# The delta-rule branch's short convolution and Silu, moved from its head loop into the input projection

## What is computed

```
proj = h @ w_in                                   # c_qkv: 3 x 1024 columns of it
qkv = jax.nn.silu(causal_short_conv(c_qkv, gdn_conv))
q_c = l2norm(qkv[..., :C_KEY] by head) * (C_DK ** -0.5)
k_c = l2norm(qkv[..., C_KEY:2 * C_KEY] by head)
v_c = qkv[..., 2 * C_KEY:]
o_c = gated_delta_rule(q_c, k_c, v_c, log_a_c, beta_c)

def causal_short_conv(x, w):                      # 4 taps along the tokens, one weight per channel
    xp = jnp.pad(x, ((0, 0), (kw - 1, 0), (0, 0)))
    return sum(xp[:, j:j + t_len] * w[j] for j in range(4))
```

## Time and profile before

| | us |
|---|---|
| median of 3 runs | 4563.6 |
| runs | 4560.57 to 4564.49 |
| span of the profiled execution | 4562.1 |
| TensorE busy | 4115.5 (90%) |
| VectorE busy | 2743.6 (60%) |
| ScalarE busy | 1845.1 (40%) |
| GpSimd busy | 747.8 (16%) |

### The profile page before, as it was taken

One profiled execution on the slowest core, in us unless ns is written; L12 is line 12 of the kernel. 1 busy time (PEld: TensorE's weight loads), 2 busy tenths in 40 slices (PEclk: granted clock), 3 DMA queues, 4 the chain that ended last, 5 costly groups with the idle time before them and its releaser, 6 DMA issues. The chain is left out here.

```text
span 4562.1 us, 66543 instructions
## 1 busy us (share of the span) xinstructions
PE 4115.5 (90%) x26381; PEld 3202.9 (70%) x26381; DVE 2743.6 (60%) x3549; ACT 1845.1 (40%) x3376; POOL 747.8 (16%) x831
## 2 busy tenths in 40 slices
PE   7999889889988979999999999688689968999997
PEld 1888667668856767888888786465378854788786
DVE  1413777651277756555655654687577756666789
ACT  0312465531145643222222332787566623433533
POOL 0200400020040011000101200576212112222001
PEclk9999999999999989999999999799799989999998
DMA  7434411134331122332323232222301038224232
GB/s 268 163 110 156 145 61 49 55 128 151 111 136 58 49 107 79 102 120 85 128 93 117 95 120 79 66 67 76 112 31 53 25 128 315 88 102 157 103 128 79
DMA packets 257763, 489.79 MB, mean 107 GB/s; under 512 B 33992, under 2 KB 70056, under 8 KB 257212
## 3 DMA queue, kind: packets, MB, share of 16 engines
q1 hardware_dynamic: 257472, 485.80, 30.5%
HBM read 345.74 MB, written 140.00 MB: 106 GB/s over the span
## 5 line engine op out<-in xcount | busy, mean ns | idle before, releaser
L1028 DVE TENSOR_TENSOR p_tl<-spare,p_th 128x1024 fp32r<-128x1024 f32 x156 | 199.4, 1279 | 362.6 <-ACT p_th L900 362.6
L900 ACT CAST p_th<-spare 128x1024 fp32r<-128x1024 f32 x156 | 163.6, 1049 | 570.4 <-PE p_ps L852 570.4
L316 PE MATMUL p_ps<-p_wh,hi 128*128 128x512 f32 x896 | 352.7, 394 | 5.8 <-DVE p_wl L484 5.8
L316 PE MATMUL p_ps<-p_wl,hi 128*128 128x512 f32 x896 | 350.6, 391 | 0.0
L316 PE MATMUL p_ps<-p_wh,lo 128*128 128x512 f32 x896 | 350.5, 391 | 0.0
L852 PE MATMUL p_ps<-p_th,p_xh 128*128 128x512 f32 x784 | 310.6, 396 | 2.0 <-DVE p_tl L1028 2.0
L852 PE MATMUL p_ps<-p_th,p_xl 128*128 128x512 f32 x784 | 310.3, 396 | 0.0
L852 PE MATMUL p_ps<-p_tl,p_xh 128*128 128x512 f32 x784 | 310.3, 396 | 0.0
L852 PE MATMUL p_ps<-p_xh,p_th 128*128 128x512 f32 x672 | 266.2, 396 | 1.0 <-DVE p_tl L1028 1.0
L852 PE MATMUL p_ps<-p_xl,p_th 128*128 128x512 f32 x672 | 265.3, 395 | 0.0
L852 PE MATMUL p_ps<-p_xh,p_tl 128*128 128x512 f32 x672 | 264.1, 393 | 0.0
(11 more groups left out here) (485 smaller groups left out, 10551.4 us busy)
## 6 DMA issues: line engine op xcount, KB each, us to landing
spare<-w_in SPq DMA_DIRECT2D x56, 1024.0 KB, 5.5
p_raw<-w_in SPq DMA_DIRECT2D x40, 1024.0 KB, 5.9
pn_dram<-p_stg SPq DMA_DIRECT2D x128, 256.0 KB, 2.1
p_dram<-p_stg SPq DMA_DIRECT2D x112, 256.0 KB, 2.1
m_w<-w_mod SPq DMA_DIRECT2D x12, 2048.0 KB, 11.5
pt_dram<-p_stg SPq DMA_DIRECT2D x96, 256.0 KB, 2.2
zm_ogm<-pn_dram SPq DMA_DIRECT2D x48, 512.0 KB, 10.1
zu_raw<-w_up SPq DMA_DIRECT2D x16, 1024.0 KB, 5.4
```

What stands on the lines that cost most here:

```text
L316: mm = pe.matmul(ps[:, u, :], lhsT, rhs, start=(kk == 0 and q == 0), stop=(kk == KD - 1 and q == 2))
L900: act.copy(th[:, g % 2], (R11, T, R21, R12, R22, R11, R21)[i][:, 2 * u:2 * u + 2]).then_inc(s_hi, 1)
L1028: dve.tensor_tensor(tl[:, g % 2], (R11, T, R21, R12, R22, R11, R21)[i][:, 2 * u:2 * u + 2], th[:, g % 2], ALU.subtract).then_inc(s_lo, 1)
```

## The change

The convolution and Silu of the 24 (stream, head) pairs become 24 jobs inside the projection, behind units 0, 3, 6 and 9 of groups 6 to 12 (from unit 6 of group 6 to unit 3 of group 12). A job loads one 128x1024 row block from `pt_dram` into `rows`, does tap 0 on ScalarE, taps 1 and 2 on VectorE, tap 3 on GpSimd (a multiply in place and an add), Silu on ScalarE behind the second unit after it, and stores the block back. Its result lies in `C.low`, so what was there goes to `low_dram` and is loaded back at the end. The weights' columns are made in the modulations and kept in `C.cw`. The delta branch loads finished rows, in two buffers. The narrow columns are loaded and split in the projection, behind the rows, before its chain of sums.

```diff
 # modulations: ScalarE, VectorE lose the narrow split, SP its two loads; added:
+            sp.dma_start(cr[:], ins["gdn_conv_2"][0].rearrange("j (s p) -> (j s) p", p=P)).then_inc(s_cr, 16)
+            pe.wait_ge(s_cr, 16)
+            pe.transpose(psC[:], cr[:], C.ident[0:96, 0:96]).then_inc(s_cc, 1)
+            dve.wait_ge(s_cc, 1)
+            dve.tensor_copy(C.cw[:].rearrange("p j s h -> p (j s h)"), psC[:])
 # seven_products
+    PAD, JOBS = 16, 3 * C_HEADS
+        rows = sb("rows", [P, PAD + SEQ])
+        cv = C.low
+        conv_q = [q for q in range(NQ) if groups[q]["conv"] is not None]
+        spots = [(q, p) for q in range(conv_q[0] + 1, NQ) for p in (0, 3, 6, 9)][2:2 + JOBS]
+        job_at = {UN * q + p: n for n, (q, p) in enumerate(spots)}
+        weight = lambda n, tap: C.cw[:, tap, n // C_HEADS, n % C_HEADS:n % C_HEADS + 1]
+        taken = lambda tap: rows[:, PAD - 3 + tap:PAD - 3 + tap + SEQ]
 # SP, behind the head gains' loads
+                sp.dma_start(narrow[:, :, 0:RANK], wv[:, :, B_GK:B_GK + RANK]).then_inc(s_narrow, 16)
+                sp.dma_start(narrow[:, :, RANK:2 * RANK], wv[:, :, C_A:C_A + 2 * C_HEADS]).then_inc(s_narrow, 16)
 # SP
+            def load_rows(n):
+                if n % C_HEADS == 0:
+                    for b in range(SG):
+                        sp.wait_ge(s_st[b], 16 * ((PLAIN + 16 * (conv_q[n // C_HEADS] + 1)) // SG))
...
+                else:
+                    sp.wait_ge(s_cv, n)
+                r = groups[conv_q[n // C_HEADS]]["out"]
+                sp.dma_start(rows[:, PAD:], r[n % C_HEADS * P:(n % C_HEADS + 1) * P, :]).then_inc(s_rl, 16)
+            def store_rows(q, p):
+                n = job_at.get(UN * q + p)
+                if n is None:
+                    return
+                if n + 1 < JOBS:
+                    load_rows(n + 1)
+                sp.wait_ge(s_cs, n + 1)
+                r = groups[conv_q[n // C_HEADS]]["out"]
+                sp.dma_start(r[n % C_HEADS * P:(n % C_HEADS + 1) * P, :], cv[:]).then_inc(s_cst, 16)
+            sp.wait_ge(s_eA, 2 * NB // 2 + 2)
+            sp.dma_start(C.low_dram, cv[0:2 * RANK, :]).then_inc(s_low, 16)
             for q in range(NQ):
                 for i, freed in ((2, ((1, 8), (3, 10))), (4, ((0, 12),)), (5, ((2, 14),)), (6, ())):
+                    if (q, i) == (spots[0][0], 2):
+                        load_rows(0)
+                    for p in {2: (0, 3), 4: (6,), 5: (9,), 6: ()}[i]:
+                        store_rows(q, p)
                     for j in range(4):
                         store(q, i, j)
...
+            sp.wait_ge(s_cst, 16 * JOBS)
+            sp.dma_start(cv[0:2 * RANK, :], C.low_dram).then_inc(s_low, 16)
+            sp.wait_ge(s_low, 32)
 # ScalarE; behind the first two unit_hi: act.copy(narrow_hi[:], narrow[:])
+            def first_tap(n):
+                act.wait_ge(s_rl, 16 * (n + 1))
...
+                    act.wait_ge(s_cst, 16 * n)
+                act.activation(cv[:], taken(0), ACT.Identity, scale=weight(n, 0)).then_inc(s_tap, 1)
+            def rows_activated(n):
+                act.wait_ge(s_cv, n + 1)
+                act.activation(cv[:], cv[:], ACT.Silu).then_inc(s_cs, 1)
                 unit_hi(g + 2)
+                if g - 2 in job_at:
+                    rows_activated(job_at[g - 2])
                 if u == 1:
...
+                if g in job_at:
+                    first_tap(job_at[g])
 # GpSimd; head_gains(q, p) are the four tiles of unit p
+            def last_tap(n):
+                pool.wait_ge(s_tapD, n + 1)
+                pool.tensor_scalar(taken(3), taken(3), weight(n, 3), None, ALU.mult)
+                pool.drain()
+                pool.tensor_tensor(cv[:], cv[:], taken(3), ALU.add).then_inc(s_cv, 1)
             for q in range(NQ):
                 gain = groups[q]["gain"]
+                for p in range(UN):
+                    if p - 1 in (5, 9, 11) and gain is not None:
+                        head_gains(q, p - 1)
+                    if UN * q + p in job_at:
+                        last_tap(job_at[UN * q + p])
                 if gain is not None:
+                    head_gains(q, UN - 1)
 # VectorE; behind the first two unit_lo: narrow_lo = narrow - narrow_hi. In the loop, last:
+            def middle_taps(n):
+                dve.wait_ge(s_tap, n + 1)
+                for tap in (1, 2):
+                    e = dve.scalar_tensor_tensor(cv[:], taken(tap), weight(n, tap), cv[:], ALU.mult, ALU.add)
+                    if tap == 1:
+                        dve.drain()
+                e.then_inc(s_tapD, 1)
+                if g in job_at:
+                    middle_taps(job_at[g])
 # gated_delta: taps, silu, conv_v, conv_qk and all their calls and waits go; the turns read the loaded rows
-            pe.transpose(ps[:, 2, 0:96], cr[:], C.ident[0:96, 0:96]).then_inc(s["conv_cols"], 1)
             def load(h):
+                if h >= 2:
+                    sp.wait_ge(s["tokens"], 3 * (h - 1))
                 for q in range(3):
                     r0 = T_C + q * D + h * P
-                    sp.dma_start(raw[:, q, PAD:PAD + SEQ], C.pt_dram[r0:r0 + P, :]).then_inc(s["raw"], 16)
+                    sp.dma_start(cv[:, h % 2, q], C.pt_dram[r0:r0 + P, :]).then_inc(s_cv[h % 2], 16)
             load(0)
-            sp.wait_ge(s["conv"], 1)
-            sp.wait_ge(s["conv_v"], 1)
             load(1)
+                    pe.wait_ge(s_cv[g % 2], 48 * (g // 2 + 1))
                     for c in range(NCK):
-                        mm = pe.transpose(chunk(6, c), cv[:, step, c * CK:(c + 1) * CK], C.ident[:])
+                        mm = pe.transpose(chunk(6, c), cv[:, g % 2, step, c * CK:(c + 1) * CK], C.ident[:])
```

More of the change, by code:

```diff
@@ L139, in _ @@
                              .rearrange("p (a b) -> p a b", a=4)).then_inc(s_lv, 16)
-            wv = ins["w_in_2"][0].rearrange("(k p) n -> p k n", p=P)
-            with nc.allow_non_contiguous_dma("4 KB of channel gains each; 64-byte rows, 128 KB in all"):
+            with nc.allow_non_contiguous_dma("4 KB of channel gains each"):
                 sp.dma_start(C.mix_scale[:, 0, :], ins["ln_mix_pre_2"][0].rearrange("(k p) -> p k", p=P)).then_inc(s_late, 16)
@@ L624, in seven_products @@
         xh[5], xl[5] = sb("xh5", [P, KH, CH], F32R), sb("xl5", [P, KH, CH], F32R)
+        ms = sb("ms", [P, NT])
+        rs = sb("rs", [P, NT])
+        with ExitStack() as early:
+            narrow = sb("narrow", [P, KD, 2 * RANK], F32, early)
+            narrow_hi = sb("narrow_hi", [P, KD, 2 * RANK], F32R, early)
+            narrow_lo = sb("narrow_lo", [P, KD, 2 * RANK], F32R, early)
+        rows = sb("rows", [P, PAD + SEQ])
+        cv = C.low
         wh, wl = (xh[4], xh[3]), (xl[4], xl[3])
@@ L728, in _ @@
                 sp.dma_start(on[:], ins[name][0].partition_broadcast(P)).then_inc(s_on, 16)
+            wv = ins["w_in_2"][0].rearrange("(k p) n -> p k n", p=P)
+            with nc.allow_non_contiguous_dma("64-byte rows, 128 KB in all"):
+                sp.dma_start(narrow[:, :, 0:RANK], wv[:, :, B_GK:B_GK + RANK]).then_inc(s_narrow, 16)
+                sp.dma_start(narrow[:, :, RANK:2 * RANK], wv[:, :, C_A:C_A + 2 * C_HEADS]).then_inc(s_narrow, 16)
             for kh in range(2):
@@ L929, in _ @@
             unit_hi(1)
+            act.wait_ge(s_narrow, 32)
+            act.copy(narrow_hi[:], narrow[:]).then_inc(s_nh, 1)
             act.wait_ge(s_lA, NT)
@@ L1077, in _ @@
             unit_lo(1)
+            dve.wait_ge(s_nh, 1)
+            dve.tensor_tensor(narrow_lo[:], narrow[:], narrow_hi[:], ALU.subtract).then_inc(s_nl, 1)
             dve.wait_ge(s_T, NT)
@@ L2540, in gated_delta @@
         s_st = [sem(f"head_stored{b}") for b in range(2)]
+        s_cv = [sem(f"convolved_loaded{b}") for b in range(2)]
         block = st.enter_context(nc.Block())
@@ L2678, in take_o @@
                 act.copy(o[:, h % 2, c], ps[:, 3, 0:CK]).then_inc(s["o_taken"], 1)
-            taps(0, (0, 1))
-            taps(0, (2,))
             gates()
-            for q in (0, 1, 2):
-                silu(0, q)
             for step in (-2, -1, 1, 0):
@@ L2687, in _ @@
             rows(0, 0)
-            taps(1, (0, 1))
-            taps(1, (2,))
             for step in (3, 4):
@@ L3915, in second_block @@
                 pt, pn = C.pt_dram, C.pn_dram
-                token = lambda a, c, act=None, gain=None: dict(w=w[:, a:a + D], out=pn[:, c:c + D], kind="token", act=act, gain=gain)
+                token = lambda a, c, act=None, gain=None: dict(w=w[:, a:a + D], out=pn[:, c:c + D], kind="token", act=act, gain=gain, conv=None)
                 silu = lambda j: dict(act=ACT.Silu, gain=C.onorm[j][:])
-                channel = lambda a, r, act=None: dict(w=w[:, a:a + D], out=pt[r:r + D, :], kind="channel", act=act, gain=None)
+                channel = lambda a, r, act=None, conv=None: dict(w=w[:, a:a + D], out=pt[r:r + D, :], kind="channel", act=act, gain=None, conv=conv)
```

(2 more changed lines are left out.)

149 lines of the change are left out of this document (42 added, 107 removed).

## The result

The changed kernel takes 4530.1 us (median of 4 runs, 4526.8 to 4533.4), the kernel before 4562.1 on the same chip: a ratio of 0.9929, 95% interval [0.9917, 0.9941], 32 us less. The forecast was 4563, range 4541 to 4580. The result lies outside it.

A forecast was written before the change was run, and what follows sets the result against it. TensorE bounds the projection; the delta branch leaves it partly idle. Summed -47 (delta branch) + 22 (unit 3) + 16 (unit 9 with gains) + 5.6 (unit 9 elsewhere) + 3 (small parts) = -0.4 us: 4563 median, range 4541 to 4580.

The forecast's parts named there:

- the delta branch: Taps and Silus leave this stage: 47 us less (37 to 59), of which 4.0 for each of five heads.
- the start: Start of the delta branch: gates, first rows and key masking no longer wait behind taps and Silu, 20 us less (16 to 22).
- the 7: First head of the delta branch, with more TensorE idle than steady heads: 7 us less (4 to 9).
- The floor named there: Delta branch: the seventh head, which has no taps, takes 45.0 us between system products, against 50.7 with taps.
- the job behind unit 3: Projection, groups 7 to 12: two taps delay T4, then GpSimd's multiply and add block VectorE; six jobs, 22 us more.
- the multiply: GpSimd's 128x1024 multiply by a column in each job, shown nowhere in the trace at this size, taken as 1.5 us.
- Rival 1: T4 precedes GpSimd's multiply behind unit 3: 12 us less, another 4 with tl(13) first in groups 10, 11; 4547 us; chance 0.35.
- mere sharing: If GpSimd and VectorE only shared bandwidth, without a lock, unit 3 would lose the overrun alone, some 20 us less in all.
- rival 2: GpSimd's multiply costs as much as its add or more; a visible loss from 2.3 us; 4573 us; chance 0.24.
- the wait behind unit 9 with gains: Projection, groups 8 and 9: GpSimd's last tap delays gains, stores and the next block 0; 8 us each, 16 more (10 to 22).
- The other jobs: Unit 9 elsewhere: tl(13) loses 0.7 us in groups 6, 7 and 2.1 in 10, 11, 5.6 more; units 0 and 6: 0.
- Small parts: Narrow columns, transpose and copy of conv columns, and reloading the low rows (2.1 us): together 3 us more.

The follow-up runs named there:

- e13: Changed kernel with VectorE waiting for its own taps' semaphore and draining before T4 in the six jobs behind unit 3: 4528.4 us, ratio to before 0.9923.
- e4_no_jobs: Changed kernel with none of the 24 jobs issued, so no convolution or Silu, all else kept: 4495.0 us, ratio to before 0.9852.
- e5: Changed kernel with the two jobs behind unit 9 of groups 8 and 9 moved to units 6 and 9 of group 12: 4507.5 us, ratio to before 0.9887.
- e1: Kernel before with only the two 32-byte tiles ms and rs allocated behind xh5 and xl5: 4543.0 us against 4564.2, ratio 0.9956.
- e2: Changed kernel with ms and rs back in front of xh0, all 24 jobs kept: 4545.9 us, ratio to before 0.9959.

## Why the prediction was wrong

What took the time out of the range is a term that the forecast does not have, the spacing of the matmuls; without it the change is inside. The step of its own sum that failed is the job behind unit 3.

**Right: the delta branch.** -47 forecast, -46 measured. By the first matmul of each head that puts the keys to the solved system (`d_ps<-d_Y,d_kb`), 23.4 us come up to the first head's (forecast 20 for the start and a part of the 7) and 22.5 over the five periods behind it, 3.3 to 3.6 us in each steady one (forecast 4.0) and 6.8 and 5.2 in the two at the ends. The floor named there, 45.0 us of the seventh head, was nearly reached: 46.3.

**Wrong: the job behind unit 3, +22 forecast, 2.4 measured** (six times 5.8 us for unit 5 instead of 5.4; with the 0.1 that unit 6 then takes longer, 3.2). The step that failed reads: "GpSimd wakes on the taps' semaphore while VectorE drains: the multiply goes first, T4 waits 1.5, the add then goes before tl(6)". VectorE does drain in front of T4, but the drain takes no longer than the semaphore's way to GpSimd: T4 goes first, by 10 ns, and tl(6) with it. Rival 1 had this argument ("a drain lasts as little as a semaphore's way"). The overrun of the two taps, 0.3 us, is nearly the whole cost, as the forecast's sentence on mere sharing said ("some 20 us less in all"). Rival 1 named the mechanism and the test ("missing or under 2 us"), but priced it at 1.7 us each, as it let the add in before tl(6). Nor is 1.5 us, or the multiply's length, what such an instruction waits for: behind units 0 it was kept out for 0.96 us. And where the multiply was issued first (e13) the loss was 0.9 us more and not 3.4, though T4 itself did not wait there: a T4 kept out by the multiply stands in no trace. Behind this stands the reading of the rule of the Trainium skill, SBUF — State Buffer, "Who interferes with whom", that the one which comes first keeps the other out for its whole instruction. The trace agrees for GpSimd's add of two inputs, here in group 7 of the kernel after, VectorE and GpSimd:

```profile
2410.37 3.29 DVE L1123 TENSOR_TENSOR p_tl<-spare,p_th 128x1024 fp32r<-128x1024 f32 x1 [3.05 <-ACT p_th L958]
```

```profile
2410.19 2.40 POOL L1064 TENSOR_TENSOR low<-low,p_rows 128x1024 f32<-128x1024 f32 x1
```

A tl issued 0.2 us behind the add took 3.29 us instead of 1.22. It does not agree for the multiply by a column, which kept tl out for 0.96 of its 2.85 us and let it run undisturbed afterwards. The forecast had tested the rule on an instruction of the first kind and used it on one of the second. (The 2.43 us that it took for the add are a product of two tiles in the earlier trace rows; the add took 2.40.)

**Mis-sized: the multiply**, taken at 1.5 us, takes 2.85. That is past the 2.3 us at which rival 2 was to decide, and rival 2 did not happen, since almost nobody waits for it. The Trainium skill, GPSIMD Engine Reference, "Engine selection", calls one-input work roughly line-rate; here it took longer than the two-input add, 2.40 us.

**Right: the wait behind unit 9 with gains; small: its price**, +16 forecast. The chain of head_gains, block 0, T1 and tl is the one in the trace: in group 8 block 0 leaves 22.5 us after the end of unit 9 (forecast 22.4) and TensorE goes on at 32.6 (31.4). Against e4_no_jobs the last units of the two groups are 8.2 and 8.1 us longer, where 8 stood. But the two groups cost 21.5 us with all their jobs, and e5 gets 22.3 of the projection back. The forecast lacks the unit behind the wait, at a lower clock (1.8 and 1.6 us), and a us or so in units 11.

**The other jobs.** Behind units other than 3 and outside these groups they cost about 7 us where 5.6 stood, in other places. tl(13) lost 1.8 and 2.1 us against the add in groups 6 and 7 (0.7 forecast) and almost nothing in groups 10 and 11 (2.1), where it came 1.9 and 1.5 us ahead of it; 1.6 us are the slow first unit of group 10. Small parts: +3 forecast, +4.4 from the projection's end to the end of the gated linear branch, of which 2.2 are the low rows' load; the other 2.2 are open.

**Absent: the spacing of the matmuls**, -20 us by the ratio of e1 alone, -22 in its projection. No step of the forecast speaks of it, though the earlier trace rows show 0.233 us for a matmul: it was taken as what a matmul costs. The sum by measured terms, -46 + 30 for all jobs + 4.4, is -12, and with the spacing's 22 us -34; the spans differ by 33.3. Without the spacing the change is e2, 4545.9 us, 0.9959 of before: inside the range, close to rival 1's 4547, and on the side of "faster", to which 0.35 was given. That agreement is partly luck, as errors cancel: in e2 the unit 3 jobs cost some 9 us less than rival 1 said, the gain groups 5 more and the other jobs 4 more.

## What to carry to other kernels

Compare first what cannot have changed: one stretch with no stall and no edited work, before and after. A difference there (78.40 against 76.38 us) is a second change, and it must be taken out before the first can be read. When an allocation moves, ask how the two operands of the busiest matmuls lie to each other; here an innocent 64 bytes were worth two thirds of the change. And for an instruction that is put in front of others on GpSimd, follow who stores what it delays: of 24 jobs, two cost more than the other 22 together.

## What the hardware showed that was not expected

- In this projection a stream of 128x512 matmuls with its weight loads is spaced 227 ns when the moving and the stationary tile start at the same remainder of 256 bytes in their partitions, and about 232 to 234 ns at 32, 64 or 128 bytes more. Groups 5 to 7 alone read 229 ns at 64 bytes; why they lie between is open, and so is which access collides. Distances other than 0, 32, 64, 128 and 256 bytes were not tried.
- GpSimd's multiply of 128x1024 by a column takes 2.85 us alone, its add of two tiles 2.40. The add kept a VectorE instruction with two SBUF inputs waiting to near its end (3.29 us instead of 1.22). The multiply kept it waiting for its first 0.96 us only: 1.29 to 1.89 us instead of 1.22 when issued 0.90 to 0.30 us behind it, and 1.23 from about 1 us on. Spans on GpSimd are rough; VectorE's durations beside them are the better witness.
- After a wait of 9.55 us TensorE's next 7.4 us had a granted clock of 0.74, so a part of them ran at the lower level of 1.2 GHz, as in the row of the kernel after below. After a short wait both were seen: in e2 unit 0 of group 8 took 7.25 us at 0.76 after a wait of 1.87 us, in after 5.59 us at the full clock after 1.96.

```profile
2510.00:2517.39 7.39, 7.38 (x25) 5.93 (x25) 5.91 (x6) 2.42 (x4) 2.32 (x2) 0.74 0.47 181
```
